# The last block's input norm in three parts of tokens, and one weight unit kept outside the ring

## The reference, cut to what matters

```
h = h + peer_ffn(rms_norm(h, norm_ffn), ...)      # end of the first block
x = rms_norm(h, norm_final)                       # its output: input of the second block
h2 = _rms(x, norm_g[0]) * (1.0 + sc) + sh         # input norm of the second block's first layer
a, b, g = split(h2 @ cv_w_in, 3)                  # its first matmul; then a gated convolution, 31 taps
x = x + gt * o                                    # x is needed again here
```

## Time and profile before

| | |
|---|---|
| median of 3 runs | 1220.59 us |
| profiled execution, its own time | 1220.2 us |
| its span | 1218.3 us |
| PE busy | 891.3 us (73%) |
| DVE busy | 799.5 us (66%) |
| ACT busy | 252.7 us (21%) |
| POOL busy | 312.9 us (26%) |
| HBM read | 400.32 MB, 329 GB/s over the span |
| gathers (queue q0) | 293.62 MB |
| weights and other loads of SP and ACT (queue q1) | 105.62 MB |

### The profile page before, as it was taken

How to read it: one execution, slowest core, us unless ns; L and a number is a source line. 1 busy time by engine, 2 the same in 40 slices (tenths; PEclk the granted TensorE clock), 3 DMA queues, 4 the chain that set the end, 5 groups by cost and what they waited for, 6 DMA issues and landing times.

```text
span 1218.3 us, 17344 instructions
## 1 busy us (share of the span) xinstructions
PE 891.3 (73%) x6816; PEld 677.0 (56%) x6816; DVE 799.5 (66%) x2065; ACT 252.7 (21%) x518; POOL 312.9 (26%) x284
## 2 busy tenths in 40 slices
PE   7899999876887894867344544433443499999998
PEld 7899697864675572754121311211211288888887
DVE  2576535577997767767797777777765389952411
ACT  2511111135222223121021011101100134242100
POOL 0001000143243333424444454444444000000000
PEclk9999999988897797977555655655555599999999
DMA  9878798499999999999999999999999714313230
GB/s 376 331 277 316 273 380 316 148 422 422 418 419 421 412 421 420 421 421 405 421 419 420 419 419 420 420 420 420 417 422 420 307 72 168 127 70 138 104 138 35
DMA packets 51409, 402.50 MB, mean 330 GB/s; under 512 B 5632, under 2 KB 7936, under 8 KB 9088
## 3 DMA queue, kind: packets, MB, share of 16 engines
q0 software_dynamic: 40320, 293.62, 58.6%
q1 hardware_dynamic: 10144, 105.62, 22.0%
q10 hardware_dynamic: 864, 2.16, 0.5%
HBM read 400.32 MB, written 1.05 MB: 329 GB/s over the span
## 4 chain that ended last, share of the span: by engine, by line
DMA 28%; PE 27%; DVE 8%; issue 3%; POOL 2%; ACT 2%; ACTq 0%; DVEq 0%; POOLq 0%
DMA wring<-uv_dram,arena 19%; PE ps L805 16%; DMA arena<-uv_dram,arena 9%; PE ps L533 4%; DVE arena L1380 2%; PE ps L446 2%; PE ps L830 2%; POOL wring L407 2%; DVE wring L1380 1%; PE ps L425 1%; DVE arena L1396 1%; PE ps L520 1%; POOL arena L407 1%; PE ps L861 1%; PE ps L500 1%
## 5 line engine op out<-in xcount | busy, mean ns | idle before, releaser
L533 PE MATMUL ps<-arena 128*32 128x256 f32 x1536 | 158.8, 553 | 224.8 <-DVE arena L1396 224.8
L407 POOL DMA_INDIRECT arena<-uv_dram,arena x192 | 225.8, 1176 | 347.5 <-PE ps L533 274.6
L1380 DVE CUSTOM_DVE_ANT_0 arena<-arena 128x1024 f32<-128x1024 f32 x192 | 232.5, 1225 | 94.8 <-DMA arena<-uv_dram,arena 90.1
L533 PEld LDWEIGHTS ps<-arena 128*32 128x32 f32 x1536 | 52.0, 142 | 313.5 <-DVE arena L1396 266.5
L805 PE MATMUL ps<-xn,wring 128*128 128x256 f32 x640 | 140.5, 382 | 7.6 <-ACT xn L1194 7.6
L805 PEld LDWEIGHTS ps<-xn,wring 128*128 128x128 f32 x640 | 122.5, 192 | 25.0 <-issue 8.1
L446 PE MATMUL ps<-xn,wring 128*128 128x128 f32 x1024 | 128.9, 288 | 7.3 <-DMA wring<-units_dram 5.9
L446 PEld LDWEIGHTS ps<-xn,wring 128*128 128x128 f32 x1024 | 125.0, 203 | 15.0 <-DMA wring<-units_dram 6.9
L938 ACT ACTIVATE gel<-dots 128x2 f32<-128x2 f32 x128 | 26.0, 203 | 453.7 <-DVE dots L1380 426.4
L533 PE MATMUL ps<-wring,arena 128*32 128x256 f32 x512 | 54.4, 566 | 67.7 <-DVE arena L1396 67.7
L407 POOL DMA_INDIRECT wring<-uv_dram,arena x64 | 73.9, 1155 | 99.5 <-PE ps L533 89.4
(11 more groups left out here) (246 smaller groups left out, 1110.5 us busy)
## 6 DMA issues: line engine op xcount, KB each, us to landing
wring<-units_dram SPq DMA_DIRECT2D x48, 2048.0 KB, 10.8
arena<-mod_dram POOLq DMA_DIRECT2D x24, 1024.0 KB, 8.5
arena<-uv_dram,arena POOLq DMA_INDIRECT x192, 14.2
hA<-x_t_dram SPq DMA_DIRECT2D x2, 512.0 KB, 19.5
arena<-mem_t_dram SPq DMA_DIRECT2D x1, 1024.0 KB, 12.6
arena<-keys_dram ACTq DMA_DIRECT2D x2, 512.0 KB, 6.5
...
```

The source lines that it names most:

```text
L407: pool.indirect_dma_start(ring[b], None, uv_d, bass.IndirectOffsetOnAxis(ap=idx[:, n:n + 1], axis=0)).then_inc(sem(f"row_in{b}"), 16)
L533: mm = pe.matmul(acc_ps(q)[G * c:G * (c + 1), :], lhsT=diag[:, s % 2, j, :], rhs=ring[b][:, D + 256 * c:D + 256 * (c + 1)], start=(p == 0 ...
L1380: post(V.tensor_tensor_reduce(out=ring[b][:, 0:D], in0=ring[b][:, 0:D], in1=x_rep[q % 2], scale=1.0, scalar=0.0, op0=ALU.mult, op1=ALU.add ...
```

## The change

- **A fourth place for one unit.** pq1 of the first tile goes to `w_pq1`, 16 KB a partition at R (where aq, prob, probT and ao of the attention lie), and has a slot number of its own, 3. Its load waits for xo1, the last reader of ao, where it waited for xo0. `first_x` moves to R + 6144. k of the second tile then finds slot 0 last used by xo0, and its load no longer waits for pq1.
- **The norm in parts.** Tokens 0 to 127 (part 0) are done wholly inside group 4, tokens 128 to 223 (part 1) wholly inside group 7, tokens 224 to 255 (part 2) after the last slot. Inside a group: squares at p = 5, sums at p = 7, copy and first root on ACT at p = 8, two DVE products at p = 9, second root on ACT at p = 10, one product and the first four blocks of `xn` on DVE at p = 11, the other four at p = 12, the shifts on ACT at p = 12 and 13, four blocks of `hB` on DVE at p = 13 and four at p = 14.
- **The last 32 tokens.** DVE makes both kinds of squares of its 8 blocks in two instructions of 256 columns, and one reduction over the blocks; TensorE needs one matmul with 64 columns (`last_sums`). ACT reads the sums from PSUM. DVE multiplies gains ahead of the roots, and makes products and the shift over all 8 blocks in single instructions.
- **The first matmuls by tokens.** The first half of cv_ab0 (`first_half`) runs 16 matmuls of 128 columns for tokens 0 to 127, then 16 for the other 128, where it ran 16 of 256. The second set waits for `shifted_last`.

```diff
@@
 W_SLOTS = 3
-LOAD_SLOT = ([i % 3 for i in range(len(CHAIN_UNITS[0]))] + [1 - i % 2 for i in range(len(CHAIN_UNITS[1]))]
+PQ1_SLOT = 3
+LOAD_SLOT = ([i % 3 for i in range(len(CHAIN_UNITS[0]) - 1)] + [PQ1_SLOT] + [1 - i % 2 for i in range(len(CHAIN_UNITS[1]))]
              + [i % 3 for i in range(len(LAST_UNITS))])
@@
 for _q in range(GROUPS):
-    AUX += ([f"back{_q - 1}"] if _q else []) + (["h3.0"] if _q == GROUPS // 2 else [])
+    AUX += ([f"back{_q - 1}"] if _q else []) + ([f"h3.{_q // (GROUPS - 1)}"] if _q in (GROUPS // 2, GROUPS - 1) else [])
     AUX += [f"rep{_q + 1}.{i}" for i in range(2)] if _q + 1 < GROUPS else []
-AUX += [f"back{GROUPS - 1}", "h3.1"]
+AUX += [f"back{GROUPS - 1}", "h3.2"]
 AUX_NO = {n: i for i, n in enumerate(AUX)}
@@
+H3_GROUPS = (GROUPS // 2, GROUPS - 1)
+H3_PARTS = (slice(0, P), slice(P, S - G), slice(S - G, S))
 EARLY = 2
@@
             return ap.rearrange("p a b -> p (a b)")
+        def weights(t, u):
+            slot = LOAD_SLOT[LOAD_NO[t, u]]
+            return w_pq1 if slot == PQ1_SLOT else wring[:, slot]
@@
         ao = blocks(area(R + 3072, 1024), KB)
-        first_x = blocks(area(R + 1024, 256), KB)
+        first_x = blocks(area(R + 6144, 256), KB)
+        w_pq1 = area(R, 4096).rearrange("p (k n) -> p k n", k=KB)
         pq = blocks(area(R + 4096, 1024), KB)
@@
         cT, o_norm = blocks(norm2[:, 0:512], 4), norm2[:, 512:1024]
-        h3s = norm2[:, 0:512].rearrange("p (t i n) -> p t i n", t=2, i=2)
+        h3s = norm2[:, 0:512].rearrange("p (i n) -> p i n", i=2)
+        last_sq = area(M, 512).rearrange("p (i k n) -> p i k n", i=2, k=KB)
+        last_sums = area(M + 512, 2 * G).rearrange("p (i n) -> p i n", i=2)
         M3 = M2 + 2048
@@
                     sp.wait_ge(sem("last_pairs"), FIRST_LAST[before[-1][1]] + LAST_PAIRS[before[-1][1]])
+                elif slot == PQ1_SLOT:
+                    sp.wait_ge(sem("pairs"), PAIR_NO[t, "xo1"] + 1)
                 elif before:
@@
                     a = UNITS.index(u)
-                    sp.dma_start(wring[:, slot].rearrange("p k n -> p (k n)"),
+                    sp.dma_start(weights(t, u).rearrange("p k n -> p (k n)"),
                                  units_d[a if a < UNITS.index("grp") else a - 1]).then_inc(sem(f"w_in{slot}"), 16)
@@
             def unit(t, name, src, step, ready=None, between=None):
-                w = wring[:, LOAD_SLOT[LOAD_NO[t, name]]]
+                w = weights(t, name)
                 out = pair_begin(t, name, True)
@@
                 post(mm, "aux")
-            def h3_sums(t):
...
-                pe.wait_ge(sem("h3_squares"), t + 1)
-                aux_begin(f"h3.{t}")
+            def h3_sums(part):
...
+                pe.wait_ge(sem("h3_squares"), part + 1)
+                aux_begin(f"h3.{part}")
+                n = H3_PARTS[part].stop - H3_PARTS[part].start
                 for i in range(2):
...
                         weight = gain2[:, k:k + 1].broadcast_to([P, P]) if i else ones
-                        mm = pe.matmul(aux_ps[:, i * P:(i + 1) * P], lhsT=weight, rhs=sq[:, k, :], start=(k == 0), stop=(k == KB - 1))
+                        mm = pe.matmul(aux_ps[:, i * P:i * P + n], lhsT=weight, rhs=sq[:, k, 0:n], start=(k == 0), stop=(k == KB - 1))
                 post(mm, "aux")
@@
                     tokens_back(q - 1)
-                if p == 7 and q == GROUPS // 2:
-                    h3_sums(0)
+                if p == 7 and q in H3_GROUPS:
+                    h3_sums(H3_GROUPS.index(q))
                 if p in (10, 12) and q + 1 < GROUPS:
@@
             tokens_back(GROUPS - 1)
-            h3_sums(1)
+            need(pe, "last_sums", 1)
+            aux_begin("h3.2")
+            post(pe.matmul(aux_ps[:, 0:2 * G], lhsT=ones, rhs=last_sums.rearrange("p i n -> p (i n)"), start=True, stop=True), "aux")
...
+            def first_half():
...
+                load = LOAD_NO[2, "cv_ab0"]
+                w = wring[:, LOAD_SLOT[load]]
+                pe.wait_ge(sem(f"w_in{LOAD_SLOT[load]}"), 16 * LOAD_COUNT[load])
+                p = FIRST_LAST["cv_ab0"]
+                out = last_ps(p)
+                for t in range(TT):
+                    need(pe, "shifted0", t + 1)
+                    if t:
+                        need(pe, "shifted_last", 1)
+                    for j in range(2):
+                        for k in range(KB):
+                            mm = pe.matmul(out[:, j * S + t * P:j * S + (t + 1) * P], lhsT=w[:, k, j * P:(j + 1) * P],
+                                           rhs=xn[:, k, tokens(t)], start=(k == 0), stop=(k == KB - 1))
+                post(mm, "last_pairs")
             def last_half(u, i, rhs, ready=None, between=None):
@@
                 return lambda k: need(pe, "last_squares", 4 * n + k // 2 + 1) if k % 2 == 0 else None
-            for i in range(4):
-                last_unit(f"cv_ab{i}", xn, ready=(lambda k: need(pe, "shifted", k + 1)) if i == 0 else None)
+            first_half()
+            last_half("cv_ab0", 1, xn)
+            for i in range(1, 4):
+                last_unit(f"cv_ab{i}", xn)
             last_unit("cv_g0", xn)
@@
             sum_channels("ss_m1", sq_all, S, squared(1))
-            last_unit("pl_v0", xn, ready=lambda k: need(pe, "shifted", KB + k + 1))
+            last_unit("pl_v0", xn, ready=lambda k: need(pe, "shifted", k + 1))
             for n in ("pl_v1", "pl_g0", "pl_g1"):
@@
                 go(act.copy(ysb[q % 2], acc_ps(q)), "y_tok")
-            def h3_squares(t):
...
-                need(act, "h2y", 4 * (t + 1))
-                go(act.activation(sq, hA[:, :, tokens(t)], ACT.Square), "h3_squares")
...
-            def h3_copy(t):
...
-                aux_ready(act, f"h3.{t}")
-                aux_used_wait(act, act.copy(h3s[:, t].rearrange("p i n -> p (i n)"), aux_ps[:, 0:256]), f"h3.{t}")
-                signal(act, "h3_sums")
+            def h3_squares(part):
...
+                n = H3_PARTS[part]
+                need(act, "h2y", n.stop // G)
+                go(act.activation(sq[:, :, 0:n.stop - n.start], hA[:, :, n], ACT.Square), "h3_squares")
...
+            def h3_first_root(part):
...
+                n = H3_PARTS[part]
+                aux_ready(act, f"h3.{part}")
+                both_sums = aux_ps[:, 0:2 * P].rearrange("p (i n) -> p i n", i=2)[:, :, 0:n.stop - n.start]
+                aux_used_wait(act, act.copy(h3s[:, :, n], both_sums), f"h3.{part}")
+                inverse_root(h3s[:, 0, n], rms[:, 0, n], 1.0 / D, "h3_root")
...
+            def h3_second_root(part):
...
+                n = H3_PARTS[part]
+                need(act, "h3_mean", part + 1)
+                inverse_root(both[:, 0, n], both[:, 0, n], 1.0 / D, "h3_root")
...
+            def h3_shift(part, blocks_of):
...
+                n = H3_PARTS[part]
+                need(act, "unshifted0", 2 * part + blocks_of + 1)
+                for k in range(4 * blocks_of, 4 * blocks_of + 4):
+                    ins = act.activation(xn[:, k, n], xn[:, k, n], ACT.Identity, bias=modc[:, k:k + 1])
+                if blocks_of:
+                    post(ins, "shifted0")
             def slot(s):
@@
                     repeated_tokens(q + 1, p // 2 - 5)
-                if p == 5 and q == GROUPS // 2:
-                    h3_squares(0)
-                if p == 8 and q == GROUPS // 2:
-                    h3_copy(0)
+                if q in H3_GROUPS:
+                    part = H3_GROUPS.index(q)
+                    if p == 5:
+                        h3_squares(part)
+                    if p == 8:
+                        h3_first_root(part)
+                    if p == 10:
+                        h3_second_root(part)
+                    if p in (12, 13):
+                        h3_shift(part, p - 12)
                 act.wait_ge(sem("dots"), BATCH * (s + 1))
@@
             tokens_out(GROUPS - 1)
-            h3_squares(1)
             table(True)
-            h3_copy(1)
-            inverse_root(h3s[:, :, 0], rms[:, 0].rearrange("p (t n) -> p t n", t=TT), 1.0 / D, "last_root")
-            need(act, "h3_mean", 1)
-            inverse_root(both[:, 0], both[:, 0], 1.0 / D, "last_root")
...
-            def shifted(layer):
+            aux_ready(act, "h3.2")
+            inverse_root(aux_ps[:, 0:G], rms[:, 0, H3_PARTS[2]], 1.0 / D, "h3_root")
+            h3_second_root(2)
...
+            def shifted():
                 for k in range(KB):
-                    need(act, "unshifted", KB * layer + k + 1)
-                    last = post(act.activation(xn[:, k], xn[:, k], ACT.Identity, bias=modc[:, 24 * layer + k:24 * layer + k + 1]), "shifted")
+                    need(act, "unshifted", k + 1)
+                    last = post(act.activation(xn[:, k], xn[:, k], ACT.Identity, bias=modc[:, 24 + k:25 + k]), "shifted")
                 need(act, "shifted", last)
...
-            shifted(0)
             def gate_sigmoid(k):
@@
             sums_root("ss_m1", rms[:, 0], "last_root")
-            shifted(1)
```

(62 more changed lines are left out.)

4 lines of the change are left out of this document (2 added, 2 removed).

## The result

| | before | changed |
|---|---|---|
| median of the timed runs, same chip | 1221.99 us (1220.56 to 1223.24, 6 runs) | 1213.12 us (1209.58 to 1217.92, 6 runs) |
| profiled execution (its span) | 1220.2 us (1218.3) | 1214.6 us (1212.8) |
| ratio | | 0.9934 [0.9917, 0.9952] |

The change is faster by 8 us; 13.3 had been forecast. The same kernel, run twice more on other chips, came to 0.9914 [0.9895, 0.9933] and 0.9913 [0.989, 0.9937], so 10.5 us. It falls short in all three. One run of before on the last of these chips took 2200.13 us and is left out of the ratios.

A forecast was written before the change was run, and what follows sets the result against it. DMA was taken to bound the gather, TensorE and DVE the stretch after it. From 1220.2 us, -9.3 - 4.5 + 0.5 = -13.3 gave 1206.9, as a median 1207.3; own range 1205 to 1209.5, ends 1204.6 and 1213.

The forecast's parts named there:

- The seam, -9.3: From the last group's addition to cv_ab0's first half done: ends 9.3 us earlier, between 4.1 and 11.0 by clock.
- B: Rival in the seam: TensorE stays at the low clock through `first_half`, gaining only 4.1 there; 1212.5 us, chance 0.12.
- The k unit, -4.5: Gather: k's earlier load takes 2.10 MB out of the full DMA stage, gaining 4.5 us, between 0 and 5.0.
- Rival A: Gather: the k unit gives nothing, as the second tile's chain sets the pace up to 560; 1211.8 us, chance 0.13.
- The roots in groups 4 and 7, +0.5: Gather slots: added roots, blocks and sums delay the next gathers, mostly absorbed; charged 0.5 us, bounds 0 and 12.8.
- The 7: Group 4: the ring is about 7.0 us late by slot 77, less than the 11 us of queue.
- D: Rival in groups 4 and 7: delays not absorbed, DMA stands, the k unit's gain is lost; 1224.1 us, chance 0.05.
- Rival C: Groups 4 and 7: a table switch costs about twice its row, group 4 12.1 late; 1210.8 us, chance 0.05.
- the bound of 12.8: Groups 4 and 7: upper bound of the roots' cost, 7.0 + 5.8 us, when every delay reaches the DMA.

The follow-up runs named there:

- e1: Before with only the k unit's early load and pq1's own slot added: 1217.4 us, ratio 0.9971.
- e12: Before with 6 extra squares on ACT in slot 82 and 8 in slot 98, ahead of the gelu: 1220.91 us, one run.
- e8: Before with extra squares on ACT ahead of the gelu, 4 in slot 82, 7 in slot 98, 10 in slot 114: 1225.77 us, one run.
- e6: e3 with the k unit's load put back as in before: 1213.14 us, ratio 0.9946.
- e3: Changed kernel with part 0's roots moved to slots 76 and 84 and its blocks one a slot from 87 to 102: 1209.97 us, ratio 0.9903.
- e4: Changed kernel with Ln and Exp in groups 4 and 7 replaced by plain activations needing no table load: 1209.77 us, ratio 0.9907.
- e2: Changed kernel with the k unit's load put back as in before: 1214.57 us, ratio 0.9949.
- the doses: Extra squares added to before in e8 and e12 to hold up ACT, making 4.4 to 10.9 us of lateness; 1225.77 and 1220.91 us.
- e5: The changed kernel itself, run again on a second chip: 1209.29 us, ratio 0.9914.
- e9: The changed kernel itself, run again on a third chip: 1210.02 us, ratio 0.9913.
- spread: The kernel of e3, run again beside e9 on the third chip: 1210.8 us, ratio 0.9908.
- e11: e3 with cv_ab0's load issued one gather earlier and 8 matmuls of its first half ahead of the summing product: 1207.09 us, ratio 0.9878.

## Why the prediction was wrong, point by point

**The seam, -9.3: right.** Measured -9.05 in the first execution, and -8.93 and -8.67 in the others (difference of spans less the offset at slot 127). Two things blur it. Before's own seam is not constant: its code took 20.84 us in before, 21.9 in e1 and e12 and 22.7 in e8, mostly since the second half of the sums ran 1.99 us in before, 2.67 in e1 and 3.21 in e8; the new one took 11.5 to 12.7 in eight executions. And the median of e6, which has the seam without the k unit, is only 6.6 us better than before (4.4 to 8.8). Its parts: the small reduction took 1.01 us, not 0.68; the first half 8.87, against 9.15; the shift was ready before it was wanted. The clock stayed low for some 4 us and then rose, so B is out. In the profiled execution all of it reached the end: from the first sigmoid on the last block took 233.4 us, as before.

**The k unit, -4.5: right in direction, too large, and not there in the first execution.** Alone it gave 3.5 by ratio and 3.3 by profile; between e3 and e6 it was 2.7 by profile. Rival A, by which it gives nothing, is out. In the first execution of the changed kernel most of the gain was gone by slot 2, and the offset at slot 71 was +0.26 instead of -4.5. That is 4.8 us, the larger part of what its gather missed. Ahead of slot 2 TensorE took 6.47 us for 32 records of L459 that it did in 3.82 before; the granted clock was 0.57 over them, and 1.00 in before. But that doesn't explain the loss: e3 and e4 fell back at slot 2 just as far (from -3.40 to -0.67 and from -5.43 to -2.81) and had it back by slot 71 (-2.78 and -5.40). The other executions of the changed kernel had -2.9 and -2.3 at slot 2, and -3.44 and -4.17 at slot 71. Why the gain stayed away in the first one is open.

**The roots in groups 4 and 7, +0.5: this is the step whose mechanism failed,** and in it one comparison: "A gather lands 13.7 us after its issue, of which its own bytes are 2.5: 11 us are queue. 7 is less than 11, so the DMA should stay fed."

The 7 was about right. Group 4 made 8.4, 6.4 and 7.1 us of lateness in three executions, and 7.7 in e2. Two things were wrong on the other side of the comparison. The first is the room: it is not 11 but 6 to 7, as the doses show. Issue to landing less the own bytes is not slack. The trace of e8_doses shows why. Behind its third dose, with the DMA at 53 GB/s from 906 to 908 us, a gather issued at 907.06 landed after

```profile
arena<-uv_dram,arena POOLq DMA_INDIRECT x1, 6.4
```

and in e5 the first gather of all, issued into an idle DMA, took 5.8. So a gather that waits for no other needs some 6 us and not the 2.5 of its bytes, and of 13.7 us only about 7.3 are queue.

The second is that before had used some of the room there: from slot 71 (676.24) to 77 (708.19) it took 31.95 us, where six slots at 4.975, the pace of slots 78 to 87, are 29.85. So it was 2.1 behind already, and the sum to compare with the room is 8.5 to 10.5. Less what stayed at slot 82 (3.3 to 4.8) that gives a room of 5 to 6 here, near the doses' figure. e4, with 2.1 + 4.5 = 6.6, lost 0.4. About 1.0 of the 2.1 may be the DMA's own, as before's gather 154 (counted from 0) landed 3.46 us behind the one ahead of it where most land 2.49 apart; without it the room comes out at 4 to 5, and why it would be smaller here than under the doses isn't shown.

Of the loss part comes back: 3.3, 2.1, 0.5 and 1.5 of 4.8, 4.8, 3.3 and 4.3 are left by slot 119 (first execution, e2, e5, e9). It comes back in steps: gathers 176, 198 and 220 of before land 1.0 us later than the pace of 2.49, and those of e5 don't. What holds those gathers up isn't shown. It was D's mechanism at D's first place, at a fraction of D's price. In group 7 the prediction held: 7.1 us of lateness at slot 120, none of it left at slot 127, as forecast; that this is because nothing is routed there any more was not tried. The lateness there was larger than the 5.8 reckoned (the sums took 5.9 us, not 4.5), and it did not matter.

Rival C, a table switch at twice its row, is out. In group 4 the first root's activation starts 0.01 us behind its load (687.02 and 687.03). The Trainium skill (ScalarE: Activation LUTs, What ACT_TABLE_LOAD costs) adds a drain of about 1.38 us to each load. By that, taking four loads away should have saved an estimated 10.6 us; e4 saved 2.8 of the mean (3.9 of the first execution), less even than the 5.1 of the loads' own rows.

**The sum.** With what was measured, -9.0, -3.5 and +0.5 to +3.3 make -9.2 to -12.0, and the changed kernel's three ratios stand for -8.1, -10.5 and -10.6. The first profiled execution is -9.05, +0.26 and +3.3: -5.5. The forecast's upper end was 1213.0, and the first median was 0.1 above it. The roots had been charged at 0.5, and the bound of 12.8 for them was left to a rival with a chance of 0.05; by the profiles the starving accounts for 2.8 us of the 7.5 that the first gather missed, and for none to 1.0 in e5 and e9. The rest of the 7.5 was missing before slot 71, where the k unit should have shown.

One reading of the forecast was incomplete, without effect on the sum: 82.3 us in 77 waits are those for rows in the buffers named arena. The same view has 25.7 us in 27 waits more for those in wring.

## What stays open

Whether the loss in group 4 shows in the median wasn't settled: side by side, changed and spread differ by less than their intervals. The first execution of the changed kernel lost the k unit's gain before slot 71, and the offsets of the early slots differ between executions by up to 2.8 us, for causes not found. In e6 and e11 one run of 256 records of the last block took 57.2 us against 55.5 elsewhere, also unexplained; it hides 1.7 us of e11's gain in its profile.
